# A decoder layer on one core: an eleventh weight buffer with gate and up ahead of down, and a mixer whose splits, high parts and last probabilities stand in another order

## The reference

```
xn = rms_norm(x, mix_norm);  parts = split(xn @ w_in)
y_rnn = gelu(rnn_y) * rg_lru(conv4(rnn_x));  y_nsa = gated sum of three attentions;  y_sc = sc_b * conv3(sc_c * sc_h)
x = x + (sum_b sigmoid(merge_b) * (y_b @ w_b_out)) @ w_out
h = silu(xt @ w_gate[e]) * (xt @ w_up[e]) * combine[:, e]
x = x + sum_e h @ w_down[e]              # xt = rms_norm(x, ffn_norm)
```

## Time and profile before

| | before |
|---|---|
| median of 3 runs | 481.46 us |
| the profiled execution | 482.39 us, of which 480.6 us span |
| PE busy | 418.0 us (87%) |
| DVE, ACT, POOL busy | 218.6, 171.2, 40.2 us |
| loaded from HBM | 145.35 MB, 305 GB/s over the span |
| chain that ended last | PE 58%, DMA 27%, DVE 9% |

### The profile page before, as it was taken

The page is one execution under the profiler, slowest core; times in us unless marked ns, Lnnn a source line. Parts: engine busy times, 40 slices in busy tenths (PEclk is TensorE's granted clock), DMA queues, the critical chain, the costliest instruction groups (busy, mean ns, idle before and its releaser), DMA issues.

```text
span 480.6 us, 6686 instructions
## 1 busy us (share of the span) xinstructions
PE 418.0 (87%) x2749; PEld 296.9 (62%) x2749; DVE 218.6 (45%) x332; ACT 171.2 (36%) x264; POOL 40.2 (8%) x66
## 2 busy tenths in 40 slices
PE   2999899999999999999999999795692956929986
PEld 2889799999887887888878743433141332503522
DVE  3757986487799995464574641101000010000201
ACT  4558418963664455244355321111100111001101
POOL 8700480000000000000003100000000000000000
PEclk9999989999999999999999999989597996968999
DMA  8987880445550477697498879999999999999992
GB/s 299 314 280 255 312 301 5 172 176 176 175 176 1 177 252 273 247 410 259 175 350 354 346 308 427 421 421 419 426 425 423 422 421 426 425 422 419 423 391 103
DMA packets 38905, 146.74 MB, mean 305 GB/s; under 512 B 2556, under 2 KB 3697, under 8 KB 28129
## 3 DMA queue, kind: packets, MB, share of 16 engines
q1 hardware_dynamic: 37280, 143.24, 76.6%
q10 hardware_dynamic: 848, 2.62, 1.6%
q0 software_dynamic: 752, 0.55, 0.5%
HBM read 145.35 MB, written 1.05 MB: 305 GB/s over the span
## 4 chain that ended last, share of the span: by engine, by line
PE 58%; DMA 27%; DVE 9%; issue 2%; SPq 2%; ACT 1%; DVEq 0%
DMA ring<-in_exp_w_down 22%; PE psum L1486 16%; PE psum L1482 10%; PE psum L1882 7%; PE psum L1691 7%; DMA odd<-in_exp_w_up 4%; PE psum L1724 4%; DVE wl L959 2%; SPq L390 2%; PE psum L1841 1%; PE psum L1826 1%; PE psum L1664 1%; DMA tok<-in_x 1%; PE psum L1643 1%; PE psum L1584 1%
## 5 line engine op out<-in xcount | busy, mean ns | idle before, releaser
L959 DVE TENSOR_TENSOR wl<-ring,wh 128x2048 fp32r<-128x2048 f32 (+1 forms) x38 | 84.8, 2237 | 30.6 <-ACT wh L651 30.5
L651 ACT CAST wh<-ring 128x2048 fp32r<-128x2048 f32 (+1 forms) x38 | 71.0, 1869 | 56.9 <-PE psum L1486 18.5
L1882 PE MATMUL psum<-ring,a_moe 128*32 128x512 f32 x256 | 39.3, 769 | 41.5 <-DMA ring<-in_exp_w_down 39.8
L1486 PE MATMUL psum<-wh,x_parts 128*128 128x512 f32 (+1 forms) x288 | 66.9, 385 | 0.0
L1486 PEld LDWEIGHTS psum<-wh,x_parts 128*128 128x128 f32 x288 | 52.8, 191 | 11.0 <-issue 0.5
L1882 PEld LDWEIGHTS psum<-ring,a_moe 128*32 128x32 f32 x256 | 10.4, 136 | 64.6 <-issue 63.6
L1482 PE MATMUL psum<-x_parts,wh 128*128 128x256 f32 x320 | 40.9, 286 | 0.0
L1427 DVE COPY yT<-psum 128x512 f32<-128x512 f32 x8 | 5.5, 692 | 76.1 <-PE psum L1882 76.1
L1482 PEld LDWEIGHTS psum<-x_parts,wh 128*128 128x128 f32 x320 | 39.6, 194 | 0.1
L1419 DVE COPY a_moe<-psum 128x256 f32<-128x256 f32 x8 | 3.4, 425 | 73.7 <-PE psum L1866 73.7
L1486 PE MATMUL psum<-wl,x_parts 128*128 128x512 f32 (+1 forms) x144 | 34.0, 378 | 0.0
(11 more groups left out here) (298 smaller groups left out, 614.6 us busy)
## 6 DMA issues: line engine op xcount, KB each, us to landing
ring<-in_exp_w_down SPq DMA_DIRECT2D x32, 1024.0 KB, 15.8
ring<-in_w_in SPq DMA_DIRECT2D x12, 2048.0 KB, 7.7
odd<-in_exp_w_gate SPq DMA_DIRECT2D x16, 1024.0 KB, 15.4
odd<-in_exp_w_up SPq DMA_DIRECT2D x16, 1024.0 KB, 17.5
a_att<-in_exp_w_gate SPq DMA_DIRECT2D x8, 1024.0 KB, 13.7
a_att<-in_exp_w_up SPq DMA_DIRECT2D x8, 1024.0 KB, 15.7
a_rnn<-in_exp_w_gate SPq DMA_DIRECT2D x4, 1024.0 KB, 20.7
a_rnn<-in_exp_w_up SPq DMA_DIRECT2D x4, 1024.0 KB, 21.9
```

Source lines behind the costliest of these rows:

```text
L651: a.copy(high, src).then_inc(hi_ready, 1)
L959: signal(v.tensor_tensor(low, src, halves(m, wh)[1].bitcast(fp32), ALU.subtract), lo_ready, m + 1)
L1486: ins = t_.matmul(bank(name)[:, 0:n], xp[hf][:, k, i * P:(i + 1) * P], wv[:, k, :], start=start, stop=stop)
L1882: ins = t_.matmul(xo[e * SLOTS:(e + 1) * SLOTS, hf, :], hT[:, c, e * SLOTS:(e + 1) * SLOTS], wd[e // E2][:, e % E2, c, hf * CB:(hf + 1) * ...
```

## The change

- SBUF: an array `mix` of 6144 elements per partition takes the place of `yT` and `wbd` and holds 2048 more in front. Its first 4096 are `odd_down`, an eleventh buffer: the first two experts' down weights of odd groups go there, so they overlap `wbd` and the recurrent branch's part of `yT`. The room is taken from the scratch of GpSimd's DMA descriptors, 8192 to 2048 bytes.
- Loads: group 1's first two down blocks are loaded in the mixer. Down of group g is asked for in two parts: the first half when down g-2 is done, the second when down g-1 is. The last group's first half goes ahead, the rest in three pieces behind down 6.
- PE in the experts: gate and up of group it+1 stand ahead of down of group it. In the last group the first two experts' down stands ahead of the other two's.
- Mixer: DVE's split of piece 8 behind the normalization of q and k; in each product, and in the first output pass, all of high x high ahead of high x low; unit 3's transposes ahead of the gate gb2, its weighted sum behind it, with ACT's and DVE's copies moved along.
- The ffn gain goes to a place of its own in `a_att`, loaded behind unit 3's output; GpSimd's fourth product waits for the first one-hot (`hot_t0`), and DVE waits for that product before it writes `posx`.

```diff
-         + ["ga2_0", "ga2_1", "gb2_0", "gb2_1"] + fills_of_unit(3) + [f"p2_{i}" for i in range(4)]
+         + ["ga2_0", "ga2_1"] + fills_of_unit(3)[:-1] + ["gb2_0", "gb2_1"] + fills_of_unit(3)[-1:] + [f"p2_{i}" for i in range(4)]
...
+        mix = sb("mix", [P, SLOT // 2 + 2 * CT * P + 3 * CT * S])
+        wbd = mix[:, SLOT // 2:SLOT // 2 + 2 * CT * P].rearrange("p (i c q) -> p i c q", i=2, c=CT)
+        yT = mix[:, SLOT // 2 + 2 * CT * P:].rearrange("p (b c s) -> p b c s", b=3, c=CT)
+        odd_down = mix[:, 0:SLOT]
...
                 if name == "sc":
                     odd_half(3, 0)
+                    down_half(1, 0, True)
+                if name == "w2":
+                    sp.wait_ge(yl_ready, 1)
+                    down_half(1, 1, True)
...
-            for g in range(1, NG - 2):
+            def down_next(g):
+                if g > 1:
+                    sp.wait_ge(down_done, (g - 1) * 2)
+                    experts(g, 4, g % 2 == 1)
+                sp.wait_ge(down_done, g * 2)
+                experts(g, 5)
+            gate_up_next(1, FIRST)
+            gate_up_next(2, FIRST[:2])
+            down_next(1)
+            gate_up_next(2, FIRST[2:])
+            down_next(2)
+            for g in range(3, NG - 1):
                 gate_up_next(g, FIRST)
-                sp.wait_ge(down_done, g * 2)
-                experts(g, 4)
-                experts(g, 5)
-            gate_up_next(NG - 2, FIRST[:2])
-            sp.wait_ge(down_done, (NG - 2) * 2)
-            experts(NG - 2, 4)
-            experts(NG - 2, 5)
-            gate_up_next(NG - 2, FIRST[2:])
+                down_next(g)
+            down_first(NG - 1, True)
             sp.wait_ge(down_done, (NG - 1) * 2)
-            down_by_row(NG - 1)
+            down_last(NG - 1, True)
...
+                if i == 3:
+                    pool.wait_ge(hot_t0, 1)
...
             gates(2, 0)
+            turned(3)
             splits(27)
             y_high(1, (y_sc_ready, 1))
             splits(28)
             gates(2, 1)
-            turned(3)
             output(3)
...
-            splits(9)
-
             dve.wait_ge(qk_root, 1)
...
+            splits(9)
             for t in range(TT):
                 full(dve, f"qT{t}")
...
             splits(26)
+            turned(3)
+            splits(27)
             y_low(1)
-            splits(27)
-            turned(3)
...
+                    pe.wait_ge(hi_ready, m + 1)
+                    w = halves(m, wh)[1]
+                    for t in range(TT):
+                        tile_pass(hf, t, w, yh, True, False)
+                    pe.wait_ge(yl_ready, i + 1)
+                    for t in range(TT):
+                        ins = tile_pass(hf, t, w, yl, False, False)
...
+            pe.wait_ge(xh_ready, 4 + 2)
+            for t in range(TT):
+                out_pass("wo0", 0, t, 0, (xh,))
             pe.wait_ge(mT_low, 2)
-            for load in ("wo0", "wo1"):
...
+            for t in range(TT):
+                ins = out_pass("wo0", 0, t, 0, (xl,))
...
+                if not final:
+                    pe.wait_ge(xg_act, it + 2)
+                    pe.wait_ge(xg_dve, it + 2)
+                    gate_up(not odd_group, nth if odd_group is False else nth + 1)
                 pe.wait_ge(hT_copied, it + 1)
...
-    nc = bacc.Bacc("TRN2", target_bir_lowering=False, num_devices=1, dynamic_dma_scratch_size=8192)
+    nc = bacc.Bacc("TRN2", target_bir_lowering=False, num_devices=1, dynamic_dma_scratch_size=2048)
```

168 lines of the change are left out of this document (97 added, 71 removed).

## The result

| | before | changed |
|---|---|---|
| median, runs of one session | 482.11 us (4 runs, 480.86 to 484.3) | 476.81 us (4 runs, 476.13 to 477.71) |
| span of the profiled execution | 480.6 us | 474.4 us |
| TensorE (PE) busy | 418.0 us | 414.7 us |
| first gate and up matmul | 276.00 | 273.36 |
| start of down 6 | 451.75 | 452.52 |

The ratio of the times is 0.9867, with a 95% interval of 0.9828 to 0.9906. The forecast was 477.1 us in a range of 473.5 to 480.5. The changed kernel is faster by 1.3%, a little more than the 0.9% that the sum gave. The experiments show that the total was forecast better than its terms.

A forecast was written before the change was run, and what follows sets the result against it. TensorE's program was taken to bound the kernel up to 276 us and weight bytes after it. Mixer 3.0 plus experts 1.35 gave 4.35 us off the 481.46 us median: 477.1 us, range 473.5 to 480.5.

The forecast's parts named there:

- The two stages: Whole kernel: TensorE's program sets the end up to 276 us, bytes behind it at 2.477 us per MiB.
- T6: Landing of group 6's down weights, forecast at 454.95 us less the mixer's gain.
- (a): Mixer, split of piece 8 behind the q and k normalization: gain 2.2 us, 1.8 from order and 0.4 from clock.
- (b): Mixer, product 0 starting with the high parts: a 0.8 us stall goes, DVE's split is late next, gain 0.2 us.
- (c): Mixer, unit 3's transposes ahead of gb2: a 1.0 us stall goes, gain 0.9 us (0.5 to 1.0).
- (d): First output pass, high parts first: fewer matmuls ahead of the wait for a bank, loss 0.9 us.
- (e): GpSimd's last product waits for the first one-hot, so DVE's one-hot is not slowed: gain 0.6 us.
- The experts: Expert groups: 2 MiB less behind 280 us saves 4.95 us, a PE-bound tail takes back 3.6, gain 1.35 us.
- The mixer kept less: Rival: mixer stalls shift rather than go and down 6 is slowed; 480.9 us, chance 0.15.
- Tail by bytes: Rival: the last group is bound by bytes, so all 4.95 us stay; 473.5 us, chance 0.12.
- Hole: Rival: the weight queue runs dry before group 3's gate and up loads, costing 2.9 us; 480.0 us, chance 0.09.
- the rival of the small scratch: Rival: with 2048 bytes GpSimd's ten small loads wait for one another and delay its convolution; 492.7 us, chance 0.06.

The follow-up runs named there:

- split_back: Changed kernel with DVE's split of piece 8 put back ahead of the normalization of q and k; span 475.1 us, shortest execution 476.83 against 476.13.
- split_alone: Kernel before with one edit, the split of piece 8 behind the normalization of q and k; ratio 0.9975, median 482.01 us against 483.24.
- out_back: Changed kernel with the first output pass as before; ratio to the kernel before 0.9851, shortest execution 475.03 us.
- hot_back: Changed kernel with GpSimd's fourth product free to start before the first one-hot; its one execution took 478.71 us.
- mixer_only: Kernel before with the five mixer edits and nothing else; ratio 0.9954, median 481.26 us.
- free: Changed kernel with the last two down blocks loaded into a free buffer without waiting for down 6; ratio 0.9877, median 476.22 us.
- experts_only: Changed kernel with all five mixer edits undone; ratio to the kernel before 0.9923, median 479.07 us.
- free_side: Changed kernel, last two down blocks loaded early into a free buffer and last down in one piece on four column groups; ratio 0.9854, median 475.93 us.
- no_last: Changed kernel with the last 2 MiB of down weights neither loaded nor waited for; 21.9 us from down 6 to the end.
- best3: Changed kernel with old first output pass, last down blocks in a free buffer, next group's transposes between scatter halves; ratio 0.9839, median 475.48 us.

## Why the prediction was right, and where it was not

**The two stages.** Right. The end of the mixer passed through to group 6 with nothing lost: T6 was forecast at 454.95 less the mixer's gain, with the measured 2.64 that is 452.3, and it came at 452.52. The price per MiB was forecast at 2.477 and measured at 2.476.

**(a)** 2.2 forecast, 2.44 read, and yet the step was wrong in its parts. "1.8 of order and 0.4 of clock" compared a new start at 60.4 (measured 60.39) with 62.20, the start in an execution whose clock had fallen. At full clock the old start is 61.15. The order is worth 0.8 (split_back) to 1.0 us (split_alone); the other 1.5 are a fall that an execution of before may or may not have. The step "behind the 2.14 us rest the granted clock falls" took one execution for the rule: behind 2.15 us in split_back it stayed at 1.00.

**(b)** 0.2 forecast, 0.05 read. The mechanism was right (DVE's split is late next), the new wait is 0.69 and not 0.55.

**(c)** 0.9 forecast, 0.55 read, inside the stated bounds. I had 0.1 for the bank that ScalarE frees, it was 0.25, and the rest went to the rows around it, a tenth here and there.

**(d)** 0.9 loss forecast, 0.88 read, 0.9 to 1.1 by out_back, and the wait 1.73 for 1.7. Edits to save a wait of 0.2 us cost 0.9, since only what lies ahead of the longest wait is free.

**(e)** 0.6 forecast, 0.67 read, and hot_back shows the cause.

**The experts.** 1.35 forecast, 3.56 read. The term for the tail was mis-sized: I had T6 + 24.3, and it was T6 + 21.9. The failing step is "two of them take as long, so cutting the last down in two halves costs 2 x 3.64 = 7.28". One set does take as long (461.61 to 465.23), but the two, on different column groups, overlap, and the second starts 1.75 us behind the first: 5.31 us. That is 1.97 of the 2.4. The transposes took 1.98 instead of 2.41, since h is ready earlier and PE waits 0.52 us for one instruction of DVE where it waited 0.91 for two. A second number missed without effect: the last bytes land near 465.2, T6 + 12.7, not + 10.7. The queue, empty when they are asked for at 456.2, carries 165 GB/s in 456:460 and 343 in 460:464, not 423 at once. PE loads weights from the last of the three at 465.53, so what was forecast as 2.7 us to spare was 0.3, and the queue fell idle 10 us before the end and not 13.

**The rivals.** The mixer kept less (2.64 of 3.0, of which 1.5 are the clock and 1.1 the order; 1.4 in mixer_only), so part of that rival was true, and a gain in the tail made up for it. Tail by bytes: no (free). Hole: none. GpSimd was delayed, as the rival of the small scratch has it: it waited twice for some 5.6 us ahead of its small loads:

```profile
21.47 0.93 POOL L624 DMA_DIRECT2D rw<-in_router_group_w  x1 [5.66 <-issue]
27.97 0.91 POOL L625 DMA_DIRECT2D rw<-in_router_expert_w  x1 [5.58 <-issue]
```

Its last load is out at 29.97 and not 19.67. With two such waits and not ten it stays 25 us ahead of the convolution at 54.93. In experts_only (2048 bytes) the same two waits are 5.99 and 5.46 us, in mixer_only (8192 bytes) there are none; that it is the scratch and not another part of the experts' change was not tested alone.

**Taken together** the forecast of 477.1 met 476.81 by terms that missed both ways: 0.4 too much in the mixer, 2.2 too little in the experts, and 482.11 for the kernel before in that session where the sum went off 481.46. The gain was forecast at 4.35 us; it is 5.3 between the medians, 4.7 between the shortest executions and 6.2 between the profiled ones, of which 1.5 are the clock. Its range and its side were right; its closeness is in part luck.

## What to carry to other kernels

When a stall disappears in a trace, ask which clock the rows behind it ran at. The gain of the order and the gain of the clock are two things, and only the first is in every execution. Compare shortest executions as well as medians when the times come in steps. Where PE must wait long for bytes, give it part of the work first even if that cut costs it order: 1.7 us of order was cheaper than a rest of 4.4 us, which cost 2.7 us behind it on top. Where the rest is short (1.2 us in free_side), look at the single executions before cutting: two of the four there beat every one of free, the other two none. And ahead of a wait that another engine ends, put as much of PE's work as has its operands, since only that part is free.

## What was not expected of the hardware

- Matmuls on two column groups and then on the other two are not serial: the first set takes 3.6 us (461.61 to 465.23 in the changed kernel), both 5.3 us, with the second 1.75 us behind the first, whether its weights are waited for, are not, or come earlier (the changed kernel, no_last, free).
- A wait of 2.14 or 2.15 us on PE left the clock at 1.00 in split_back, and behind it the clock fell in before and experts_only; at 266 us a stretch with no wait over 0.31 us saw the fall in best3 and no_last, and not in the changed kernel with the same rows. Which it will be could not be read from these traces and stays open.
- An empty queue took time to reach its rate: 165 GB/s over the four us in which three loads of 2 MiB in all were issued, 343 in the next four, with 423 in steady state. These loads are also cut finer than the others, and no run here separates the two.
